# Thirteen gate tiles as three products of rounded operands, with GpSimd forming the remainders

## The reference, cut to what matters

```python
proj = h @ p['w_in']
q, k, v, o, gates, u, ga, gb = jnp.split(proj, IN_SPLITS, axis=-1)
...
y, xf = s5_scan(u, ...)                        # the state-space branch reads u
merged = jax.nn.sigmoid(ga) * (h_a @ p['w_pA']) + jax.nn.sigmoid(gb) * (h_b @ p['w_pB'])
out = merged @ p['w_out']
```

## Time and profile before

| | us |
|---|---|
| median of three runs | 1665.42 (1665.17 to 1665.93) |
| the profiled execution, its own time | 1662.37 |
| its span in the trace | 1660.6 |
| TensorE busy in the whole span | 1564.6 (94%) |
| VectorE busy in the whole span | 688.0 (41%) |
| u block, first u product to the last engine's end | 48.4 to 85.9 |
| state-space stage | 86.4 to 277 |

### The profile page before, as it was taken

One profiled execution on the slowest core, in us unless ns is written; L12 is line 12 of the kernel. 1 busy time (PEld: TensorE's weight loads), 2 busy tenths in 40 slices (PEclk: granted clock), 3 DMA queues, 4 the chain that ended last, 5 costly groups with the idle time before them and its releaser, 6 DMA issues. The chain is left out here.

```text
span 1660.6 us, 35159 instructions
## 1 busy us (share of the span) xinstructions
PE 1564.6 (94%) x15950; PEld 1042.2 (63%) x15950; DVE 688.0 (41%) x1430; ACT 372.7 (22%) x717; POOL 114.8 (7%) x173
## 2 busy tenths in 40 slices
PE   5999999999999999889987999999999999999993
PEld 2456665889898987888983444444454444445451
DVE  7878994323334244677532222222112222222214
ACT  5254434232424233544330000000000000000001
POOL 0000000000000000400012011110011111110000
PEclk9999999999999999999978999999999999999996
DMA  9355455021212110625148999999999999999985
GB/s 390 125 165 162 134 174 216 6 97 54 74 52 77 39 44 37 224 102 216 39 169 327 424 415 415 416 414 423 415 416 415 416 415 414 415 416 419 420 368 171
DMA packets 58138, 420.39 MB, mean 253 GB/s; under 512 B 11444, under 2 KB 18740, under 8 KB 28292
## 3 DMA queue, kind: packets, MB, share of 16 engines
q1 hardware_dynamic: 51460, 392.76, 58.7%
q0 software_dynamic: 6528, 25.37, 5.0%
HBM read 391.55 MB, written 24.42 MB: 250 GB/s over the span
## 5 line engine op out<-in xcount | busy, mean ns | idle before, releaser
L2002 PE MATMUL bank<-place,hT 128*32 128x384 f32 x3120 | 257.7, 490 | 10.0 <-issue 10.0
L2002 PE MATMUL bank<-ring_tail,hT 128*32 128x384 f32 x3024 | 247.2, 486 | 0.0
L2002 PEld LDWEIGHTS bank<-place,hT 128*32 128x32 f32 x3120 | 106.7, 111 | 155.2 <-issue 153.7
L2002 PEld LDWEIGHTS bank<-ring_tail,hT 128*32 128x32 f32 x3024 | 102.7, 110 | 140.0 <-issue 139.2
L2089 DVE TENSOR_TENSOR xT<-sq,bank 128x384 f32<-128x384 f32 x48 | 23.7, 549 | 367.2 <-PE bank L2002 342.1
L2060 DVE SCALAR_TENSOR_TENSOR hT<-bank,gvr,xT 32x256 f32<-32x256 f32 (+1 forms) x192 | 92.1, 480 | 201.0 <-PE bank L2020 198.5
L2046 ACT ACTIVATE sq<-bank 128x384 f32<-128x384 f32 x48 | 20.1, 491 | 692.0 <-PE bank L2002 692.0
L2020 PE MATMUL bank<-place,xT 128*32 128x256 f32 x2304 | 126.8, 379 | 0.0
L2020 PE MATMUL bank<-ring_tail,xT 128*32 128x256 f32 x2304 | 126.6, 379 | 0.0
L1618 PE MATMUL bank<-a_h,w_h 128*128 128x320 f32 x320 | 102.5, 320 | 12.0 <-DVE w_l L1719 9.5
L2020 PEld LDWEIGHTS bank<-place,xT 128*32 128x32 f32 x2304 | 78.2, 110 | 48.0 <-issue 3.4
(11 more groups left out here) (405 smaller groups left out, 2290.2 us busy)
## 6 DMA issues: line engine op xcount, KB each, us to landing
place<-w_e_dram SPq DMA_DIRECT2D x97, 1536.0 KB, 24.2
ring_tail<-w_e_dram SPq DMA_DIRECT2D x95, 1536.0 KB, 24.5
place<-w_ada_dram SPq DMA_DIRECT2D x12, 2048.0 KB, 10.0
place<-w_qk_dram SPq DMA_DIRECT2D x4, 2048.0 KB, 8.1
place<-w_vo_dram SPq DMA_DIRECT2D x4, 2048.0 KB, 8.4
xT<-w_gate_dram POOLq DMA_DIRECT2D x7, 1024.0 KB, 6.6
place<-w_pAB_dram SPq DMA_DIRECT2D x4, 1536.0 KB, 6.3
hT<-gates_dram SPq DMA_DIRECT2D x4, 1280.0 KB, 6.1
```

The costliest lines, as they stand in the source:

```text
L2002: mm = pe.matmul(PS[bank + j][TJ * g:TJ * g + TJ, 0:FC], x[:, e % 2, j, 2 * c + k, :], w[:, k, FC * g:FC * g + FC], start=(c == 0 and k == 0),
```

## The change

It makes the thirteen gate tiles of the state-space stage with three products of rounded operands, as the mLSTM stage does with its chunks.

- `pe_gate`: 48 matmuls of 320 columns a tile in place of 16 of 512 and 128 columns.
- The rows are rounded at the start of the u block by ScalarE (eight activations into `h_high`), no longer at the start of the mLSTM stage. Their remainders overwrite `hT`, so each waits for the product of the last u tile that reads the same slice (`u_done` now counts the eight steps of that tile). GpSimd forms them: five in the u block, three at the start of the state-space stage.
- The gate weights come tile by tile (13 loads of 512 KB). ScalarE rounds a tile (`round_gate`) ahead of its wait for the gate tile before; GpSimd forms the remainder in place (`split_gate`) behind the store and the load in its own queue.
- One staging tile (`rsb`) in place of two.
- The decay rows (`R`, four exponentials on four partitions) move from the start of the state-space stage to ScalarE's queue in the u block, ahead of the last `out_u`, and read `Mx` in place of `negM`.
- For room, `negM`, `Kt` and `kd` move to other partitions of `spare`; VectorE copies `negM` once more in the mLSTM stage.
- The eight roundings and eight remainders of the rows go from the start of the mLSTM stage, and counts of semaphores follow.

```diff
-        plan.append((ar["w_u"], "u_done", 4, 1))
+        plan.append((ar["w_u"], "u_done", 3 + KD, 1))
...
+        H_SPLIT = KD + 1
+        SPLITS = KD + NU_S5
+
+        def load_gate(pool, u):
+
+            pool.dma_start(gw[u % 2][:].rearrange("p k n -> p (k n)"), ar["w_gate"][u]).then_inc(sem(f"gate_w{u % 2}"), 16)
+
+        def round_gate(act, u):
+
+            if u < NU_S5:
+                act.wait_ge(sem(f"gate_w{u % 2}"), 16 * (u // 2 + 1))
+                if u >= 2:
+                    act.wait_ge(sem("gate_done"), u - 1)
+                act.activation(gw_high[u % 2][:], gw[u % 2][:], ACT.Copy).then_inc(sem("split_high"), 1)
+
+        def split_gate(pool, u):
+
+            if u < NU_S5:
+                pool.wait_ge(sem("split_high"), KD + u + 1)
+                pool.tensor_tensor(gw_low[u % 2][:], gw[u % 2][:], gw_high[u % 2][:].bitcast(F32),
+                                   ALU.subtract).then_inc(sem("split_low"), 1)
+
+        def split_rows(pool, ks):
+            for k in ks:
+                pool.wait_ge(sem("split_high"), k + 1)
+                pool.wait_ge(sem("u_done"), 3 + k + 1)
+                pool.tensor_tensor(h_low[:, k, :], hT[:, k, :], h_high[:, k, :].bitcast(F32),
+                                   ALU.subtract).then_inc(sem("split_low"), 1)
 
         def pe_gate(pe, u, banks):
 
-            pe.wait_ge(sem(f"gate_w{u // 2 % 2}"), 16 * (u // 4 + 1))
+            pe.wait_ge(sem("split_low"), H_SPLIT + u)
             if u:
                 pe.wait_ge(sem("gate_sig"), u)
             for k in range(KD):
-                w = gw[:, u // 2 % 2, k, (u % 2) * P:(u % 2 + 1) * P]
-                pe.matmul(PS[banks[0]][:, :], w, hT[:, k, 0:LAT], start=(k == 0), stop=(k == 7))
-                mm = pe.matmul(PS[banks[1]][:, 0:CTX], w, hT[:, k, LAT:TOK], start=(k == 0), stop=(k == 7))
+                for x in range(2):
+                    t = slice(x * TH, (x + 1) * TH)
+                    for i, (w, h) in enumerate(((gw_high, h_high), (gw_high, h_low), (gw_low, h_high))):
+                        mm = pe.matmul(PS[banks[x]][:, 0:TH], w[u % 2][:, k, :], h[:, k, t], start=(k == 0 and i == 0),
+                                       stop=(k == 7 and i == 2))
             mm.then_inc(sem("gate_done"), 1)
...
-        def act_gate(act, u, banks, stage):
-
+        def act_gate(act, u, banks):
+
+            round_gate(act, u + 1)
             act.wait_ge(sem("gate_done"), u + 1)
-            if u >= 2:
-                act.wait_ge(sem(f"gate_out{u % 2}"), 16 * (u // 2))
-            act.activation(stage[:, 0:LAT], PS[banks[0]][:, :], ACT.Sigmoid)
-            act.activation(stage[:, LAT:TOK], PS[banks[1]][:, 0:CTX], ACT.Sigmoid).then_inc(sem("gate_sig"), 1)
-
-        def store_gate(pool, u, stage):
+            if u:
+                act.wait_ge(sem(f"gate_out{(u - 1) % 2}"), 16 * ((u - 1) // 2 + 1))
+            act.activation(rsb[:, 0:TH], PS[banks[0]][:, 0:TH], ACT.Sigmoid)
+            act.activation(rsb[:, TH:TOK], PS[banks[1]][:, 0:TH], ACT.Sigmoid).then_inc(sem("gate_sig"), 1)
+
+        def store_gate(pool, u):
 
             pool.wait_ge(sem("gate_sig"), u + 1)
-            pool.dma_start(ar["gates"][u], stage).then_inc(sem(f"gate_out{u % 2}"), 16)
-            if u % 2 and u // 2 + 2 < (NU_S5 + 1) // 2:
-                load_gate(pool, u // 2 + 2)
+            pool.dma_start(ar["gates"][u], rsb[:]).then_inc(sem(f"gate_out{u % 2}"), 16)
+            if u + 2 < NU_S5:
+                load_gate(pool, u + 2)
+            split_gate(pool, u + 2)
...
@@ the u block, GpSimd
-                pool.wait_ge(sem("xpos_out"), 16)
-                for half in range(2):
-                    load_gate(pool, half)
+                load_gate(pool, 0)
+                split_rows(pool, range(5))
+                split_gate(pool, 0)
@@ the u block, TensorE
-                    mm.then_inc(sem("u_done"), 1)
+                        if m == 3 or k == 7:
+                            mm.then_inc(sem("u_done"), 1)
@@ the u block, ScalarE
+                act.wait_ge(sem("xpos_out"), 16)
+                for k in range(KD):
+                    act.activation(h_high[:, k, :], hT[:, k, :], ACT.Copy).then_inc(sem("split_high"), 1)
                 act.wait_ge(sem("gate_abs"), 1)
...
-                for m in range(4):
+                for m in range(3):
                     out_u(m)
+                act.wait_ge(sem("m_ready"), 1)
+                for d in range(2):
+                    act.activation(R[:, 2 + d, 0:LAT], Mx[:, d, 0:LAT], ACT.Exp, bias=gpar[:, 4 + d:5 + d], scale=-1.0)
+                    ins = act.activation(R[:, 4 + d, :], cum[:, d, :], ACT.Exp, scale=-1.0)
+                ins.then_inc(sem("rows_ready"), 1)
+                round_gate(act, 0)
+                out_u(3)
@@ the state-space stage, GpSimd
+                load_gate(pool, 1)
+                split_rows(pool, range(5, KD))
+                split_gate(pool, 1)
                 for u in range(NU_S5):
-                    store_gate(pool, u, gstage[u % 2])
+                    store_gate(pool, u)
@@ the state-space stage, ScalarE
-                act.wait_ge(sem("m_ready"), 1)
-                for d in range(2):
-                    act.activation(R[:, 2 + d, 0:LAT], negM[:, d, 0:LAT], ACT.Exp, bias=gpar[:, 4 + d:5 + d])
-                    ins = act.activation(R[:, 4 + d, :], cum[:, d, :], ACT.Exp, scale=-1.0)
-                ins.then_inc(sem("rows_ready"), 1)
                 gate()
@@ the mLSTM stage, ScalarE
-                for k in range(KD):
-                    act.activation(h_high[:, k, :], hT[:, k, :], ACT.Copy).then_inc(sem("split_high"), 1)
                 round_weights(0)
@@ the mLSTM stage, VectorE
-                for k in range(KD):
-                    dve.wait_ge(sem("split_high"), k + 1)
-                    dve.tensor_tensor(h_low[:, k, :], hT[:, k, :], h_high[:, k, :].bitcast(F32),
-                                      ALU.subtract).then_inc(sem("split_low"), 1)
                 split_weights(0)
...
-                v(dve.tensor_copy(high.bitcast(F32R), negM[:]))
-                v(dve.tensor_tensor(rest, negM[:], high, ALU.subtract))
+                v(dve.tensor_copy(rest, negM))
+                v(dve.tensor_copy(high.bitcast(F32R), rest))
+                v(dve.tensor_tensor(rest, rest, high, ALU.subtract))
```

More of the change, by code:

```diff
@@ L127, in program @@
         negM_at = nc.sbuf_base
-        negM = sb("negM", [H, 2, TOK], F32, acts)
+        negM_room = sb("negM_room", [P, 2, TOK], F32, acts)
+        negM = spare[96:96 + H, 2048:2048 + 2 * TOK].rearrange("h (d t) -> h d t", d=2)
+        gw_high1 = nc.alloc_sbuf_tensor_at("gw_high1", [P, KD, P], F32R, offset=negM_at)
         negM_parts = nc.alloc_sbuf_tensor_at("negM_parts", [P, 2, TOK], F32R, offset=negM_at)
@@ L351, in program, with add_gate_tile @@
         s5p = sb("s5p", [P, 5, GN], F32, s5)
+        s5bc_at = nc.sbuf_base
         s5bc = sb("s5bc", [P, 4, GN, GC], F32, s5)
+        gw_high = (nc.alloc_sbuf_tensor_at("gw_high0", [P, KD, P], F32R, offset=s5bc_at), gw_high1)
+        gw, gw_low = [], []
+        def add_gate_tile(stack):
+            at = nc.sbuf_base
+            gw.append(sb(f"gw{len(gw)}", [P, KD, P], F32, stack))
+            gw_low.append(nc.alloc_sbuf_tensor_at(f"gw_low{len(gw_low)}", [P, KD, P], F32R, offset=at))
+        add_gate_tile(s5)
         s5d = sb("s5d", [GC, GN], F32, s5)
@@ L654, in out_u @@
                 def out_u(m):
-                    act.wait_ge(sem("u_done"), m + 1)
+                    act.wait_ge(sem("u_done"), m + 1 if m < 3 else 3 + KD)
                     if m >= 2:
@@ L711, in _ @@
                                                  gpar[:, 4 + d:5 + d] if s == 0 else 0.0, ALU.max, ALU.max))
-                v(dve.tensor_scalar(negM[:], Mx[:], -1.0, None, ALU.mult))
+                v(dve.tensor_scalar(negM, Mx[:], -1.0, None, ALU.mult))
                 v(dve.tensor_tensor(cum[:], cum[:], Mx[:], ALU.add))
@@ L727, in program @@
             bbz = sb("bbz", [P, 2, 2, QG, GC], F32, st)
-            Kt = sb("Kt", [GC, QG, (2 * L - 1) * GC], F32, st)
-            kd = sb("kd", [GC, QG, GC], F32, st)
+            KT = QG * (2 * L - 1) * GC
+            Kt = spare[96:96 + GC, 0:KT].rearrange("p (g n) -> p g n", g=QG)
+            kd = spare[96:96 + GC, KT:KT + QG * GC].rearrange("p (g c) -> p g c", g=QG)
+            add_gate_tile(st)
             T = sb("T", [P, QG, P], F32, st)
@@ L878, in gate @@
                     u = next(gates)
-                    act_gate(act, u, (4, 5), gstage[u % 2])
+                    act_gate(act, u, (4, 5))
                 def turned_coefficients(q, r):
@@ L983, in _ @@
                         v(dve.memset(V[:, r, :, JL + 1:JL + 2], 0.0))
[L985 removed]
+                    v(dve.tensor_tensor(kd, bc(s5d[:, g].unsqueeze(2), [GC, QG, GC]),
                                         bc(ident[0:GC, 0:GC].unsqueeze(1), [GC, QG, GC]), ALU.mult))
@@ L1125, in project_features @@
```

(8 more changed lines are left out.)

6 lines of the change are left out of this document (removed).

## The result

The changed kernel takes 1686.05 us (median of four runs, 1684.28 to 1686.79); the kernel before takes 1665.3 us beside it. The ratio is 1.0126, 95% interval 1.0113 to 1.0138: 20.8 us slower, where the prediction said 1680.5, 15 us slower. The profiled execution took 1686.27 us with a span of 1684.5, 23.9 us more than that of before. New are L288 (ScalarE rounds a weight tile), L294 and L301 (GpSimd's remainders of weights and of rows).

The account below looks back on a forecast made before the run. TensorE set the stage's length with VectorE close behind; slowed by GpSimd's remainders, VectorE would decide. 1662.4 us profiled + 15.3 at the last outputs = 1677.7, plus 3.0 to the median, given as 1680.5 us; range 1651 to 1687.

Parts of the forecast that it names:

- The disputed term: State-space stage and u block: VectorE loses up to 2.4 us per GpSimd remainder; less 15%, 22.4 us over eleven remainders.
- The rows at 838.65: Profile before: GpSimd tensor-tensor beside VectorE instructions with one operand in PSUM, neither longer; evidence for VectorE not being slowed.
- The front: U block and before the first gate tile: block ends at 95.9 us (+10.0), tile 0 starts at 102.8 (+13.7).
- The stage: State-space stage: VectorE takes 142.5 us from 118.1 plus 22.4 for remainders, ending at 283.0 us.
- It ends at 283.0, and the last outputs start there: End of the state-space stage: VectorE decides; last outputs start at 283.0 instead of 267.66 us, +15.3 us.
- half of it, at some 4 us, is there about 2 us ahead of need: Gate tile loads of the state-space stage: halved from 1024 KB, landing in some 4 us, early enough.
- up to 2 us for the last outputs: Last outputs of the state-space stage: TensorE at 1.2 GHz after idling, an upper end not in the sum.
- The lock plus the slow clock: Rival: +15.3 + 2 and up to 3 us of GpSimd waiting in front, +20, 1686 us; chance 0.12.
- VectorE isn't slowed: Rival: GpSimd's remainders cost VectorE nothing; -14.4 us (1651), or -9.6 (1656) if GpSimd waits; chance 0.25.
- 2.7 us of stalls: Rival without slowing, state-space stage: second tiles of the quarters stall TensorE 1.5 + 3 x 0.4 us.
- The sum of the tile: Gate products: 48 at 0.147 us, 7.04 us a tile in place of 8.65, saving 1.61 us each.
- the 20.9 us: Gate products on TensorE: saving over thirteen tiles, if TensorE is what is waited for.

Follow-up runs that it names:

- run 3: The change with every weight remainder followed by a second GpSimd subtraction of the rounded weights: 1719.35 us, ratio 1.0302 to the kernel before.
- run 9: The kernel before with 36 added, unused GpSimd subtractions of two 128x384 SBUF inputs: 1674.31 us, ratio 1.0050.
- run 10: The kernel before with 36 added, unused GpSimd multiplications of one 128x384 SBUF input by a constant: 1663.49 us, ratio 0.9992.
- Run 2: The change with only the thirteen weight remainders cut to 64 of 1,024 columns, row remainders whole: 1686.82 us, ratio 1.0115 to the kernel before.
- run 1: The change with all GpSimd remainders cut to a sixteenth of their columns, ScalarE filling the rest: 1678.18 us, ratio 1.0068 to the kernel before.
- run 6: The change, remainders whole, with gate loads ahead of the stores and SyncE's last 2 MB loads held back: 1682.91 us, ratio 1.0115 to the kernel before.
- run 5: The change with all GpSimd remainders cut to a sixteenth, gate loads ahead of stores, SyncE's last 2 MB loads held: 1663.97 us, ratio 1.0000 to kernel before.

## Why the prediction was right, and where its sum was not

**Direction and mechanism held.** The disputed term was what a remainder costs VectorE. The prediction took the upper end less 15%, 2.04 us; a remainder of 2.35 us cost VectorE's instruction 2.1 us (2.90 for 0.83, and 3.52 for 1.35 in run 3), and the eleven of the stage 23.4 us together, where 22.4 was forecast. The single row that it went by, a copy that took 0.86 us in place of 0.19, was half of a rule that goes both ways. The rule weighed there (the Trainium skill, SBUF — State Buffer, section "SBUF: two separate sides") is borne out by runs 3 and 9, for a GpSimd instruction with two inputs, and by run 10 for one input. The remainder itself took 2.35 us at least and 2.54 at the median, where 2.4 was taken. The rows at 838.65, which spoke against it, had an operand of VectorE in PSUM.

**The front.** Forecast for the u block's end: 95.9 us, +10.0. VectorE, the last engine in it, ends at 94.14, and the next block's first product starts at 94.69 in place of 86.39, +8.3. Tile 0 was forecast at 102.8 and began at 100.29: the turns between the two engines in front were over-counted. But it ran 10.0 us in place of 7.0, at a granted clock of 0.70, and so ended at 110.3, where 109.8 was forecast. VectorE's first wait for lags ended at 119.97, forecast 118.1. Run 2 less run 1 puts 8.6 us on the eight row remainders.

**The stage.** VectorE's last states: forecast 283.0, measured 286.5, of which 1.9 us are the late start and 1.0 the remainders; the last 0.6 was not taken apart. In run 6's profiled execution 284.2. A quarter: forecast about 48, measured 47.9.

**The step that was mis-sized** is the end: "It ends at 283.0, and the last outputs start there". In the change they start 4.9 us behind VectorE, at 291.42. Under it lies the sentence on the load, "half of it, at some 4 us, is there about 2 us ahead of need". The last load was issued only at 271.55, behind the remainder and the store in GpSimd's queue, and took 6.2 us; over the stage a gate load took 4.7 us at the median and up to 7.9, and ScalarE waited for seven of them, 41 us in all. So the last tile left TensorE 2.7 us idle. The other half is the clock: the tile ran 2.5 us longer than 7.04, at 0.72. The prediction priced such a thing at up to 2 us for the last outputs and left it out of the sum; it came one tile earlier. Without the two, 5.3 us, the last tile would have ended at 286.2 by estimate, level with VectorE's states. The two buffers now hold raw tile and remainder one after the other, so a load starts only behind the products. These 4.9 us, and the 3.5 us of VectorE, make +23.8 in place of +15.3 at the last outputs; from there to the GLU product it is 15.4 us in place of 15.1.

**What was luck.** 1686.05 us lies 1 us inside a range of 36 us, which also holds no change and 14 us of gain. It agrees with the rival *The lock plus the slow clock*, 1686, whose clock term did appear; but that rival's 3 us of GpSimd waiting in front did not (the front was 1.7 us shorter than forecast), and the late load, which did, is not in it. Its number is therefore in part luck. The sum itself is 0.2 us off: 1662.4 + 15.3 + 3.0 is 1680.7, not 1680.5.

**The rival that was half right.** "VectorE isn't slowed" gave 1651 to 1656. With the exclusion nearly gone the result was still not that: run 1 took 1678, and with the loads mended 1664. The prediction counted 2.7 us of stalls there; in run 5 TensorE still waits 3.3, 3.7 and 3.5 us in three quarters for ScalarE's copies, which stand behind a gate load, 10.5 us together. Part of that can be ScalarE's filling copies, which no run takes away. What was missed is that two limits lay almost level: 18 us of VectorE, and the loads right behind it. Taking away the first gives 10 us (run 1), the second some 2 (run 6, not clear of noise), both 21 (run 5).

**The sum of the tile.** The products are 0.147 us apart and 7.04 us a tile at the full clock, as forecast; none of the 20.9 us was seen in the total.

## What to carry to other kernels

Work put on an idle GpSimd is not free for VectorE when it reads SBUF, with one input or two: price it at up to its length as VectorE's own time (2.1 us for a remainder of 2.35). Here VectorE does the same work in half (1.2 us for GpSimd's 2.35). When a change makes the bounding engine faster, list the second and the third bound beside it before booking the gain, and test them in pairs: the early loads were worth some 2 us alone and 11 us once VectorE was free. A buffer that holds both the raw and the derived form ties the next load to the end of the last use; look then at what else is issued in that very moment.

## What the runs showed of the hardware

A load of 512 KB that lands in 3.7 us at the least took 13.8 and 13.5 us (runs 1 and 2) when 4096 KB of another queue were issued within 0.6 us of it. With the same loads 0.8 and 2.4 us behind it, it took 6.2 (the change), and with them held back 6.1 (run 5). GpSimd's subtraction of two 128x384 inputs took 0.99 us at least and 1.43 at the mean beside a busy VectorE, so the exclusion stretches both engines: VectorE lost 0.56 us for each. Of its instructions with all operands in SBUF every form was held: products, scans, tensor-scalars and copies. A one-input GpSimd instruction of the same size (0.51 us at least, 0.76 at the mean) cost it 0.21 us, and one that only writes (0.42 at least, 0.46 at the mean) 0.08, all of that on copies and a tensor-scalar, none on instructions with two inputs. A gate tile that began behind 2.7 us of idle time on TensorE ran at a granted clock of 0.72 and cost 2.5 us more; the last tile of run 6, behind 0.5 us idle, had a clock of 1.00 in its own window of 8.5 us.
